# Sixteen more tokens through gathered rows of U, and dense score products 368 columns wide

## What is computed

```python
q = (xt @ wq).reshape(PEER_BLOCK, PEER_HEADS, 2, PEER_HALF)
s1, s2 = ...                                   # scores against two sets of 128 keys
v1, i1 = lax.top_k(s1, 16); v2, i2 = lax.top_k(s2, 16)
top, pos = lax.top_k(cand, 16)                 # 16 of the 16 x 16 sums, for each of 8 heads
g = jax.nn.softmax(top, axis=-1)
u = expert_u[eidx]                             # 128 chosen experts per token
act = jax.nn.gelu(jnp.einsum("td,thkd->thk", xt, u), approximate=False)
out = jnp.einsum("thk,thkd->td", act * g, expert_v[eidx])
```

## Time and profile before

| | us |
| --- | --- |
| median of three runs | 1619.09 |
| the profiled execution | 1615.73 |
| its span | 1614.0 |
| TensorE busy | 1576.6 |
| VectorE busy | 1143.7 |
| GpSimd busy | 1076.3 |
| ScalarE busy | 623.3 |

### The profile page before, as it was taken

How to read it: one execution, slowest core, us unless ns; L and a number is a source line. 1 busy time by engine, 2 the same in 40 slices (tenths; PEclk the granted TensorE clock), 3 DMA queues, 4 the chain that set the end, 5 groups by cost and what they waited for, 6 DMA issues and landing times.

```text
span 1614.0 us, 25730 instructions
## 1 busy us (share of the span) xinstructions
PE 1576.6 (98%) x9029; PEld 1435.2 (89%) x9029; DVE 1143.7 (71%) x2362; ACT 623.3 (39%) x961; POOL 1076.3 (67%) x550
## 2 busy tenths in 40 slices
PE   7999989999999999999999999999999999999998
PEld 6987888888999999999999999988888878888888
DVE  6868554302969999759989985467675777767766
ACT  3223762211333333445555555433333333333331
POOL 5444313453469888676666665788898789988863
PEclk9999999999999999999999999999999999999999
DMA  6211312321469889689999998999999999999961
GB/s 213 87 63 71 112 44 95 132 104 52 140 225 316 300 304 297 240 277 337 336 349 338 334 355 285 352 365 353 360 358 364 349 356 360 358 355 355 369 248 47
DMA packets 172517, 417.78 MB, mean 259 GB/s; under 512 B 13088, under 2 KB 97696, under 8 KB 167328
## 3 DMA queue, kind: packets, MB, share of 16 engines
q1 hardware_dynamic: 133856, 257.52, 44.8%
q0 software_dynamic: 36864, 134.23, 24.3%
q10 hardware_dynamic: 1728, 25.17, 4.0%
HBM read 360.25 MB, written 56.62 MB: 258 GB/s over the span
## 4 chain that ended last, share of the span: by engine, by line
PE 68%; DVE 4%; DMA 1%; issue 1%; POOL 1%; ACT 0%; SPq 0%; DVEq 0%; POOLq 0%
PE s_psum L1451 30%; PE s_psum L1501 29%; PE s_psum L1485 5%; PE s_psum L211 1%; PE s_psum L213 1%; PE s_psum L212 1%; DMA scores<-gate_scratch 1%; DMA s_gtile<-in_v_t,s_v_row 1%; POOL s_gtile L1437 0%; DVE s_psum L1737 0%; DVE s_gtile L1735 0%; DVE s_gtile L1733 0%; POOL u_lo L1402 0%; DVE s_besti L1683 0%; DVE s_besti L1692 0%
## 5 line engine op out<-in xcount | busy, mean ns | idle before, releaser
L1402 POOL TENSOR_TENSOR u_lo<-u_raw,u_hi 128x1024 fp32r<-128x1024 f32 x222 | 534.5, 2408 | 210.1 <-ACT u_hi L1556 207.1
L1451 PE MATMUL s_psum<-hn_hi,u_hi 128*128 128x384 f32 x1024 | 347.3, 339 | 2.1 <-PEq L128 2.1
L1451 PE MATMUL s_psum<-hn_lo,u_hi 128*128 128x384 f32 x1024 | 343.2, 335 | 0.0
L1556 ACT CAST u_hi<-u_raw 128x1024 fp32r<-128x1024 f32 x254 | 263.9, 1047 | 184.1 <-PE s_psum L1501 103.7
L1501 PE MATMUL s_psum<-u_hi,s_whi 128*128 128x512 f32 x768 | 298.3, 389 | 1.6 <-ACT s_acts L1561 0.9
L1501 PE MATMUL s_psum<-u_hi,s_wlo 128*128 128x512 f32 x768 | 298.0, 389 | 0.0
L1501 PE MATMUL s_psum<-u_lo,s_whi 128*128 128x512 f32 x768 | 298.0, 389 | 0.0
L1437 POOL DMA_INDIRECT s_gtile<-in_v_t,s_v_row x128 | 213.0, 1664 | 25.1 <-issue 24.6
L1451 PE MATMUL s_psum<-hn_hi,u_lo 128*128 128x384 f32 x1024 | 198.3, 334 | 2.0 <-POOL u_lo L1402 2.0
L1451 PEld LDWEIGHTS s_psum<-hn_hi,u_hi 128*128 128x128 f32 x1024 | 193.0, 188 | 2.3 <-issue 2.3
L1451 PEld LDWEIGHTS s_psum<-hn_lo,u_hi 128*128 128x128 f32 x1024 | 193.1, 189 | 0.0
(11 more groups left out here) (313 smaller groups left out, 2798.7 us busy)
## 6 DMA issues: line engine op xcount, KB each, us to landing
u_raw<-in_u_t SPq DMA_DIRECT2D x128, 512.0 KB, 5.3
u_raw<-in_v_t SPq DMA_DIRECT2D x128, 512.0 KB, 7.1
act_scratch<-s_acts SPq DMA_DIRECT2D x128, 192.0 KB, 4.6
gate_scratch<-s_gtile ACTq DMA_DIRECT2D x12, 2048.0 KB, 9.3
scores<-act_scratch SPq DMA_DIRECT2D x32, 768.0 KB, 7.1
scores<-gate_scratch SPq DMA_DIRECT2D x32, 768.0 KB, 10.3
m_w_raw<-in_w_in SPq DMA_DIRECT2D x11, 1024.0 KB, 4.8
m_w_raw<-in_w_q SPq DMA_DIRECT2D x8, 1024.0 KB, 4.8
```

The costliest lines, as they stand in the source:

```text
L1402: pool.tensor_tensor(lo[:, s, :], raw[:, s, :], hi[:, s, :].bitcast(F32), ALU.subtract).then_inc(lo_ready[s], 1)
L1451: return pe.matmul(psU[:, s % 2, :], uu[:, s, d * P:(d + 1) * P], hh[:, d, P:T], start=start, stop=stop)
L1556: act.copy(hi[:, s, :], raw[:, s, :]).then_inc(hi_ready[s], 1)
```

## The change

The last 16 tokens of block 3 (`XT`) leave the dense score pass. Its products are 368 columns wide (`DS`), and the Gelu too; the stored activations of these tokens are ones. Their 16 x 128 chosen rows of U are gathered instead, as 16 more gathers (`XK`) of 128 rows: partition 16 g + t takes token t and its 16 experts from 16 g on (g from 0 to 7). For this the 16 normed rows go to DRAM and come back eight times (`hn_x`, in SBUF), and so do their ids (`x_ids` to `x_row`, by ScalarE's queue). VectorE dots the 16 gathered sets with `hn_x`. ScalarE takes the Gelu, stores the result and loads it transposed (eight loads of 4-byte pieces); VectorE multiplies it into the gate weights of these tokens before loop step 46. The value pass is unchanged.

In order: six more dots of block 0 (`DOTS_M`) are made between the softmax and the turned ids, with their gathers behind the low parts 65 to 67; the turn moves from before step 68 to before step 70; the Exp moves behind step 66, the ids are stored there and loaded behind step 68. The 16 late dots are the first of the loop's 72, and GpSimd waits for the ids before the first of their gathers, behind low part 72, where six are due at once. Behind the loop 15 dots are left instead of five: seven gathers are due behind low part 120, then two behind each of 121 to 124, and `weights` stays three dots before the end.

```diff
-DOTS_1, DOTS_T, DOTS_J = 3, 16, 12
+DOTS_1, DOTS_T, DOTS_M, DOTS_J = 3, 16, 6, 12
+XT = 16
+XG = P // XT
+XK = PAIRS // XG
+DS = DT - XT
...
+            sp.wait_ge(sem["row_ready"], 2)
+            sp.dma_start(hx_dram, xn(TB - 1)[P - XT:P, :]).then_inc(sem["late_stored"], 16)
+            sp.wait_ge(sem["late_stored"], 16)
...
+            dve.wait_ge(sem["pe_tile"], bank.index[("hnT", DC - 1)] + 1)
+            me.did(dve.tensor_tensor(xn(TB - 1), xn(TB - 1), gain, ALU.mult), sem["row_ready"])
...
+        hn_x = nc.alloc_sbuf_tensor_at("s_hn_x", [P, D], F32, offset=w_at)
+        x_ids = nc.alloc_sbuf_tensor_at("s_x_ids", [P, PAIRS], U32, offset=w_at + D * 4)
...
+        in_a = DOTS_1 + (TB - 1) * DOTS_T
+        x_from = in_a + DOTS_M
+        x_till = x_from + XK
+        row_of = lambda q: (x_row, q - x_from) if x_from <= q < x_till else (u_row, q if q < x_from else q - XK)
...
+            for g in range(XG):
+                sp.dma_start(hn_x[g * XT:(g + 1) * XT, :], hx_dram).then_inc(hx_loaded, 16)
+            sp.wait_ge(ones_set, 1)
...
+                if q == x_from:
+                    pool.wait_ge(x_loaded, 16 * XG)
+                ids, c = row_of(q)
+                reached(pool, dotted[s], q // U_RING)
...
-                in_a, in_b = DOTS_1 + (TB - 1) * DOTS_T, DOTS_J * n_body
-                for start, end, before, count in ((FIRST_GATHER, EXP_AT, 0, in_a), (LOOP_A, LOOP_C, in_a, in_b),
-                                                  (LOOP_C, n_steps, in_a + in_b, PAIRS - in_a - in_b)):
+                in_b = DOTS_J * n_body
+                for start, end, before, count in ((FIRST_GATHER, EXP_AT, 0, in_a), (EXP_AT + U_AHEAD, LOOP_A, in_a, 0), (LOOP_A, LOOP_C, x_from, in_b),
+                                                  (LOOP_C, n_steps, x_from + in_b, PAIRS + XK - x_from - in_b)):
                     if n < end:
+                        if EXP_AT <= n < LOOP_A:
+                            return in_a + min(DOTS_M, 2 * (n - EXP_AT))
...
-                    return pe.matmul(psU[:, s % 2, :], uu[:, s, d * P:(d + 1) * P], hh[:, d, P:T], start=start, stop=stop)
+                    return pe.matmul(psU[:, s % 2, 0:DS], uu[:, s, d * P:(d + 1) * P], hh[:, d, P:T - XT], start=start, stop=stop)
...
+            for n in range(TURN_AT, TURN_AT + 2):
+                score(n // UR, n % UR)
 
             pe.wait_ge(found_ready, 1)
             for j in range(3):
                 for t in range(1, TB):
                     last = pe.transpose(turned[j][:, (t - 1) * P:t * P], found[:, t, j, :], ident)
             last.then_inc(all_turned, 1)
-            with pe.Fori(TURN_AT // UR, LOOP_A // UR) as it:
-                for s in range(UR):
-                    score(it, s)
+            for n in range(TURN_AT + 2, LOOP_A):
+                score(n // UR, n % UR)
...
-                act.activation(acts[:, s, :], psU[:, s % 2, :], ACT.Gelu).then_inc(act_ready[s], 1)
+                act.activation(acts[:, s, 0:DS], psU[:, s % 2, 0:DS], ACT.Gelu).then_inc(act_ready[s], 1)
...
+            for n in range(EXP_AT, LOOP_A):
+                if n == EXP_AT + 3:
+                    act.wait_ge(dve_line, TB * OPS)
+                    act.activation(found[:, :, 2, :], found[:, :, 2, :], ACT.Exp).then_inc(exp_ready, 1)
+                    act.wait_ge(x_known, 1)
+                    act.dma_start(xi_dram, x_ids[P - XT:P, :]).then_inc(x_stored, 16)
+                if n == EXP_AT + 5:
+                    act.wait_ge(x_stored, 16)
+                    for g in range(XG):
+                        act.dma_start(x_row[g * XT:(g + 1) * XT, :], xi_dram[:, g * XK:(g + 1) * XK]).then_inc(x_loaded, 16)
+                split((n + 2) // UR, (n + 2) % UR)
+                gelu(n // UR, n % UR)
...
+            steps(1)
+            for s in range(U_RING):
+                act.wait_ge(dotted[s], x_till // U_RING + (s < x_till % U_RING))
+            act.activation(x_dots[:, :], x_dots[:, :], ACT.Gelu).then_inc(x_gelu, 1)
+            act.wait_ge(x_gelu, 1)
+            act.dma_start(xa_dram, x_dots[:, :]).then_inc(xa_stored, 16)
+            steps(2)
+            act.wait_ge(xa_stored, 16)
+            for g in range(XG):
+                act.dma_start(x_acts[g * XK:(g + 1) * XK, :], xa_dram[g * XT:(g + 1) * XT, :].rearrange("t k -> k t"), allow_slow_non_contiguous=True).then_inc(xa_back, 16)
+            with act.Fori(3, n_body) as j:
...
+            dve.memset(acts[:, :, DS:DT], 1.0).then_inc(ones_set, 1)
...
+            def dot_of_pair(q):
+                late = x_from <= q < x_till
+                if q == x_from:
+                    dve.wait_ge(hx_loaded, 16 * XG)
+                dot(q % U_RING, q // U_RING + 1, hn_x[:, :] if late else hn_dot, col(x_dots if late else dots, row_of(q)[1]))
...
+            dve.tensor_copy(x_ids[:, :], expert).then_inc(x_known, 1)
...
+            for q in range(in_a, x_from):
+                dot_of_pair(q)
...
+                if step_no == DS // STEP_TOK:
+                    dve.wait_ge(xa_back, 16 * XG)
+                    dve.tensor_tensor(pair[:, 1, DS:DT], pair[:, 1, DS:DT], x_acts[:, :], ALU.mult).then_inc(x_weighted, 1)
+                    dve.wait_ge(x_weighted, 1)
...
-            first_ones = PAIRS - c0 - 3
-            for c in range(c0, PAIRS):
-                if c == c0 + first_ones:
+            last = PAIRS + XK
+            for c in range(c0, last):
+                if c == last - 3:
                     weights(0, 1)
                 dot_of_pair(c)
             for s in range(U_RING):
-                dve.wait_ge(dotted[s], PAIRS // U_RING)
+                dve.wait_ge(dotted[s], last // U_RING)
```

More of the change, by code:

```diff
@@ L358, in filled, with mixer_and_retrieval @@
         return self.at(*name)
[L361 removed]
+def mixer_and_retrieval(nc, shared, io, h_dram, e_dram, hx_dram):
     h = shared["h"]
@@ L1209, in experts_and_embedding @@
         dve_line, hn_copied = S("dve_line"), S("hn_copied")
+        ones_set, hx_loaded, x_known, x_stored, x_loaded = (S(n) for n in ("ones_set", "hx_loaded", "x_known", "x_stored", "x_loaded"))
+        x_gelu, xa_stored, xa_back, x_weighted = (S(n) for n in ("x_gelu", "xa_stored", "xa_back", "x_weighted"))
         exp_ready, found_ready, all_turned, ids_ready = (S(n) for n in ("exp_ready", "found_ready", "all_turned", "ids_ready"))
@@ L1276, in experts_and_embedding @@
         dots = sb("s_dots", [P, PAIRS])
+        x_row = sb("s_x_row", [P, XK], U32)
+        x_dots = sb("s_x_dots", [P, XK])
+        x_acts = sb("s_x_acts", [P, XT])
+        in_a = DOTS_1 + (TB - 1) * DOTS_T
+        x_from = in_a + DOTS_M
+        x_till = x_from + XK
+        row_of = lambda q: (x_row, q - x_from) if x_from <= q < x_till else (u_row, q if q < x_from else q - XK)
         besti = sb("s_besti", [P, LISTS, TOPK], U32)
@@ L1406, in gather @@
                 nonlocal pair_no
-                c, s = pair_no, pair_no % U_RING
-                if c == 0:
+                q, s = pair_no, pair_no % U_RING
+                if q == 0:
                     pool.wait_ge(rows_known, 2)
-                reached(pool, dotted[s], c // U_RING)
-                pool.indirect_dma_start(rows[s], None, io["u_rows"], bass.IndirectOffsetOnAxis(ap=u_row[:, c:c + 1], axis=0),
+                if q == x_from:
+                    pool.wait_ge(x_loaded, 16 * XG)
+                ids, c = row_of(q)
+                reached(pool, dotted[s], q // U_RING)
+                pool.indirect_dma_start(rows[s], None, io["u_rows"], bass.IndirectOffsetOnAxis(ap=ids[:, c:c + 1], axis=0),
                                         bounds_check=NK * NK - 1).then_inc(row_loaded[s], 16)
@@ L1427, in _ @@
                     gather()
-            assert pair_no == PAIRS
+            assert pair_no == PAIRS + XK
             for n in range(n_steps):
@@ L1570, in _ @@
                     gelu(it, s)
-            act.wait_ge(dve_line, TB * OPS)
-            act.activation(found[:, :, 2, :], found[:, :, 2, :], ACT.Exp).then_inc(exp_ready, 1)
-            with act.Fori(EXP_AT // UR, LOOP_A // UR) as it:
-                for s in range(UR):
-                    split(it + (s + 2) // UR, (s + 2) % UR)
-                    gelu(it, s)
+            for n in range(EXP_AT, LOOP_A):
[10 more added lines that the diff above has]
+                gelu(n // UR, n % UR)
             def steps(j):
@@ L1593, in _ @@
             steps(0)
-            with act.Fori(1, n_body) as j:
+            steps(1)
[9 more added lines that the diff above has]
+            with act.Fori(3, n_body) as j:
                 steps(j)
@@ L1651, in _, with dot @@
         def _(dve):
-            def dot(s, rounds, into):
+            def dot(s, rounds, by, into):
                 dve.wait_ge(row_loaded[s], 16 * rounds)
-                dve.tensor_tensor_reduce(rows[s], rows[s], hn_dot, 1.0, 0.0, ALU.mult, ALU.add, into)\
+                dve.tensor_tensor_reduce(rows[s], rows[s], by, 1.0, 0.0, ALU.mult, ALU.add, into)\
```

(8 more changed lines are left out.)

11 lines of the change are left out of this document (5 added, 6 removed).

## The result

The changed kernel takes 1633.59 us (median of 4 runs, 1632.93 to 1637.62) against 1618.48 us for the kernel before on the same chip (1614.69 to 1620.9): a ratio of 1.0095, 95% interval 1.0077 to 1.0112. It is 15 us slower, where 9 us faster had been forecast, with a range of 1602 to 1620. The profiled spans are 1630.8 and 1614.0 us, 16.8 apart; both profiled executions are among the shorter ones of their kernel.

The account below looks back on a forecast made before the run. TensorE, busy 98% of the span, was taken as the bound, then the DMA, then VectorE. 18.5 - 0.1 - 2.0 - 1.5 - 0.5 - 5.7 = 8.7 us off 1619.09 gave 1610.4 us, range 1602 to 1620.

Parts of the forecast that it names:

- The matmuls: Score products 368 instead of 384 columns wide: 2768 in gapless stretches save 6.67 ns each, 18.5 us in all.
- The turn: Turning of the retrieved ids: six added dots end at 694.0, covered by 1.7 us; loop step 72 starts at 703.7.
- The first late rows: Start of the loop: late gathers make step 73's one-hots late; 2.0 us lost, ends 0 and 5.
- The loop: Loop steps: 16 late dots with both operands in SBUF wait for GpSimd's low parts; 1.5 us lost, bounds 0 and 25.6.
- rival B: Loop: late dots keep meeting GpSimd's low parts and the pattern locks in; 11.7 us slower, 1631; chance 0.09.
- The transposing loads: After 24 loop steps: ScalarE's eight issues, 2.7 us, nearly fit its idle time; 0.5 us lost, upper end 3.
- The handover: Steps 120 to 127, before the value products: bytes of ten more gathered rows lose 5.7 us, ends 0 and 14.3.
- D: The DMA gives back everything: 14.3 + 4.1 against 18.5 us, 1619, no change; chance 0.09.
- Nothing of the value stage changes: Value pass after the score steps: no loss priced, its 1062 products still in one piece.
- Rival A: Score steps to value products: the added rows' cost is absorbed; 14.4 us gained, 1604.7; chance 0.23.
- C: Score pass: products don't shrink at 368 columns, 9 of 9.8 us of losses stay; 1628; chance 0.04.

Follow-up runs that it names:

- ten rows thin: The changed kernel with the last ten gathers of U 128 columns wide instead of 1024: 1622.04 us in one run.

## Why the prediction was wrong, by its steps

- **The matmuls, 18.5 us: right.** Step 72 starts at 703.46 (forecast 703.7), 24 products take 4.00 us, and the narrow products alone bring the value products 18.3 us forward.
- **The turn: step 72 on time, though not for the stated reason.** The six dots ended at 695.8 instead of 694.0, behind the turn itself, since the multiplication before them (L1821) took 2.83 us instead of the 0.69 of the earlier trace rows: it has both operands in SBUF and ran beside a low part that began at 686.09. Step 72 had room for it.
- **The first late rows, 2.0 us (0 to 5): 8.7.** The step that failed is "the eight id loads, which ScalarE issues at 0.34 us each": they took 4.52 us. That made the cut and low part 71 late, and low part 72 behind it ended at 701.2 instead of 698.7: 2.5 us late, where 0.7 had been allowed. GpSimd issued the first late gather at 701.36, and its dot started at 707.05. Landing took about as long as forecast (4.7 us and, for the second row, 5.3, against 4.6), and the ids were there in time. The second dot then met low part 73 (2.5 us), which the prediction had priced separately, and TensorE ran the next spread products at the lower clock (1.7 us), which it had not priced at all.
- **The loop, 1.5 us (0 to 25.6), and rival B: the mechanism exists, the cost doesn't.** The dots did meet low parts: 16 of them took 25.6 us instead of 19.4, so 0.4 us more for each. That is near the 0.5 of a dot that starts anywhere; "most will miss it" failed, and that it cost little was due to VectorE's slack. Only that one meeting in a step that was late anyway reached TensorE; the kernel with the late rows six dots later has dots no faster and no wait for VectorE in the loop. The result lies near B's 1631, by other causes. By the rule of the Trainium skill (SBUF — State Buffer, "Who interferes with whom") a dot with two SBUF inputs contends with a low part and one with an input in PSUM does not; the runs agree (3.65 us against 1.22). The prediction has it that the second to issue is held. Here the dot was, though its record begins 0.19 us before the low part's (708.98 against 709.17), so the records don't settle the order.
- **The transposing loads, 0.5 us (upper end 3): 7.2.** "eight issues at 0.34 = 2.7 us fit": they took 7.90 us. The price was right for one load, and wrong for eight in a row. What waited was right: the cut, the low part and the copies of gates, all behind ScalarE.
- **The handover, 5.7 us (0 to 14.3): 13.7.** It is the DMA's bytes, as forecast, at the upper end that D had. "The idle share from 980 to 1000 takes ... 6.2 us" failed: the two slices have a share of 0.63 and 0.81 now, against 0.66 and 0.72, which is 0.6 us more of work. The rows had it: the seven gathers are due behind low part 120, which ends at 990.65 in the earlier trace rows (now at 989.58), so none of them could fill the slice from 980. The 2.4 us of lead that low part 126 had didn't help either: the bytes that count are those ahead of one tile of U, and that tile is issued late because SP waits for the last store of gates. The forecast looked at GpSimd's queue and at the DMA's share, and not at SP's.
- **"Nothing of the value stage changes": 5.7.** The unpriced term. Its rows were in reach. In the kernel before (length; busy us as above; clock, DMA share, GB/s):

```profile
1040.00:1320.00 280.00, 280.00 (x1237) 231.86 (x1236) 195.37 (x119) 94.22 (x85) 235.56 (x120) 1.00 1.01 359
```

  A group is 72 products of 226.9 ns, 16.3 us, and loads four tiles and four rows of 0.524 MB and two sets of 0.786 MB, 5.77 MB: 353 GB/s, and the DMA's share is 1.01 at 359. So TensorE and the DMA are both at their limit in this stage. How the 5.7 us come about in the changed kernel is only known in part: 3.2 are longer waits for low parts (3.9 against 0.7), and 1.3 of the 3.9 fall before 1220.61, where SP issues the first h load. No run of the changed kernel moved the h loads alone.

Rival A (the handover absorbed) and C (no narrower products) fell, and D had the handover's price but not the other losses. The four losses are 8.7 + 7.2 + 13.7 + 5.7 = 35.3 us against 18.5. All but the last had been named; three sizes were off, and all three to the same side: two, the first in part, because the price of one issue was taken for eight in a row, the third because the DMA was taken to have room where no gather could use it.

## What to carry to other kernels

Count a change's small transfers by what their issue costs on the engine that issues them, in a row and not one by one, and put them one per step of a loop in which that engine has slack. Before any saving is booked, ask each later stage whether its second limit stands as high as the first: here taking 2.1 MB out of the full stretch of the value pass was worth 6 to 8 us by the ratios to the kernel before (0.991 to 0.9858, 0.99 to 0.9861). And where a tile is late, look for the wait ahead of it on the queue that loads it.

## What the runs showed of the hardware

- A DMA's issue has no fixed price on its queue. Issues of the transposing load of 4-byte pieces (256 of them each) in a row (ns, minimum, median and maximum), and of the loads of ids:

```profile
L1638 ACTq DMA_DIRECT2D s_x_acts<-late_acts_scratch x8: 447/1084/1371, 851.6 to 859.0; - x8
```

```profile
L1609 ACTq DMA_DIRECT2D s_x_row<-late_ids_scratch x8: 319/446/1293, 690.7 to 694.7; - x8
```

  One per step the transposing loads take 0.31 to 0.49. A plain load of a tile of U, 0.34 us in the loop, took 8.06 on SP's queue at the handover, against 4.17 in the kernel before and 2.78 with ten rows thin. The Trainium skill (DMA: Bandwidth & Descriptors, "Issuing engines are not separate DMA queues") calls the time that initiating a DMA takes usually small against the DMA. For one of the transposing loads the trace agrees (median 1.08 us, against 7.1 from issue to landing); but the eight issues in a row took 7.90 us of an engine that TensorE then waited for.
- The granted clock is down behind a wait of 4.8 us (0.69 from 860 to 870) as behind one of 7.0 (0.66 from 710 to 720): 16 spread products took 3.79 and 3.48 us instead of 1.78, and the next 24 products 4.33 instead of 4.00 in the first case. Behind the wait of 1.8 us in the value pass (at 1239.9) it was 1.00.
- The DMA moved 402 to 418 GB/s in stretches of 10 us with many gathers of 4 KB rows (at the handover), with a share of 1.02 to 1.04, but 348 to 359 in the value pass with 0.98 to 1.01. What makes the difference was not tested.
